# Hybrid two-layer block: buffer places on 512-byte lines, and the order of work in the four norm stretches

## The chip, the cores and the metric

One core of a Trainium2 chip runs the program. The metric is the device time of one execution in microseconds. Engines are named as in the profile: PE (TensorE matmuls), PEld (TensorE weight loads), DVE (VectorE), ACT (ScalarE), POOL (GpSimd), SP (SyncE, which issues the DMAs).

## The reference

Two transformer-like layers run one after the other on one sequence of 1024 tokens of width 1024, in float32. Each layer has this form, and each half of it ends in a norm stretch:

```
h   = rmsnorm(x, g_pre_mix);  proj = h @ w_in          # 53 (layer 1) or 54 (layer 2) column blocks of 128
y_* = mixers(proj)                                      # scan, short conv and attention; or band attention,
                                                        # gated recurrences and spatial gating
mix = (sum over branches of gate * (y @ w_branch)) @ w_out
x   = x + rmsnorm(mix, g_post_mix)                      # a norm stretch
h   = rmsnorm(x, g_pre_mlp)
x   = x + rmsnorm(mlp(h), g_post_mlp)                   # a norm stretch; hidden width 4096, or 2 x 2816 gated
```

`rmsnorm(x, g) = x * rsqrt(mean(x*x) + 1e-6) * g`, with the mean over the 1024 features of one token.

## The kernel before

**Layout.** Activations are transposed: features on the 128 partitions, tokens along the free dimension. A float32 activation block of 128 features is [128, 1024], 4096 bytes in each partition. The input of the large products is kept as a pair, `act_hi` (rounded) and `act_lo` (the rest), each [128, 8, 1024]. Other products stream `f1hh`/`f1hl` and `f2hh`/`f2hl` (the MLPs' hidden blocks), `m1h`/`m1l` and `m2h`/`m2l` (the merges of the mixers' outputs).

**Products.** A weight tile is split the same way into `w_hi` (ACT, L268) and `w_lo` (POOL, L272) from `w_raw`, which SP fetches in units of eight tiles. One tile of one output block is six matmuls on one PSUM pair: (w_hi, hi), (w_hi, lo), (w_lo, hi), each over two halves of 512 tokens. The weights stand still and the activations stream. `products` (L312) does this for whole stages. The class `TwoBlocks` (L431) does it for two output blocks by half, at chosen moments.

**How many.** Streams of 512 columns from `act_hi` and `act_lo`: layer 1's projection 53 blocks x 48 and layer 2's 54 x 48, together 5136; two output products `mix_out`, 384 each; the hidden products of the MLPs, 1536 and 2112. That makes 9552, of which 48 stand on L981. Streams from the other pairs: f1 1536, f2 1056, m1 576, m2 384, together 3552.

**Woven stages.** The projections are not stages of their own: `Woven` hands their tiles out one by one between the instructions of the mixers, by points counted in the code (`point(n)`) or by a time (`beside(us)`, with TILE_US = 1.42 for one tile). TensorE runs all of it in program order. From about 92 to 860 us the projection of layer 1 is woven with its mixers, from 1857 to 2620 us that of layer 2.

**Bridges.** Between two large products stands a norm stretch, `bridge`. It runs four times: after each `mix_out` (the first at about 1060 to 1124 us, the third at 2795 to 2857 us), after the first MLP (the second, 1802 to 1861 us), and after the second MLP (the last, which ends the program). It finishes the last two output blocks of the product before (`tail`), normalises by half of the tokens, and starts the first two blocks of the next product (`head`). For each half h and block k there is a `step(h, k)`: `add` on DVE (L519 and L520; on the last bridge L510 and L513 or L515), ACT's `act_hi` (L534), DVE's `act_lo` (L535), ACT's square (L539), then on PE the head's matmuls (L431) and the sum of the square over the features (L545). In the first half the head's second block follows two steps behind; in the second half it comes after the last step, eight tiles in a row.

The scale of a half needs the sum of the squares of all eight output blocks. ACT squares a block, POOL adds it to `squares` (L589), `half_sums` sums over the partitions on PE (L453, eight matmul records), `half_root` goes DVE (L467) and ACT (L468), and `half_spread` is DVE's reciprocal (L473) and PE's spread to all partitions (L475). For the second half these calls stand after step (0, 3), (0, 4) and (0, 6). On the last bridge they stand after (0, 2), (0, 4) and (0, 6), and there the last square is summed by PE itself, not through POOL.

The head's own scale comes the same way in L462 to L475. The evictions of its first half, `head.evicted(o, 0, ...)`, stand in DVE's and ACT's order after steps (1, 4) and (1, 5). What they do depends on the product: `relu2` (L1833, L1834, ACT L1829, L1830) on the first bridge, `first_rows` (L1926) on the second, `swiglu` (L1839, ACT L1841, L1843, L1830) on the third.

**Places.** Buffers in SBUF follow one another in the order in which they are allocated, each start rounded up to 32 bytes. The first one, `w_raw`, starts at byte 16512 of each partition. The start of a buffer modulo 512 bytes (slices of tiles and halves add multiples of 512 and change nothing):

| buffer | start | modulo 512 | modulo 256 |
|---|---|---|---|
| w_raw, w_hi, w_lo | 16512, 24704, 32896 | 128 | 128 |
| act_hi, act_lo | 43328, 76096 | 320 | 64 |
| m1h, m2h, f1hh, f2hh and their other halves | 121216 and on | 384 | 128 |
| foxks (streamed in the first attention) | 166272 | 384 | 128 |
| bandks (streamed in the band attention) | 158880 | 160 | 160 |

`sb` is the function that allocates.

Of the kernel before, what the change touches and what calls it, by code (L numbers as in the profile page):

```python
# [9 lines left out]
P = 128  # L10
# [41 lines left out]
for _name, _n in VEC_NAMES:  # L52
    VEC[_name] = sum(VEC[m][1] for m in VEC), _n
NVEC = sum(n for _, n in VEC_NAMES)


# [69 lines left out]
def _build(nc, ctx, t, out):  # L126
    def sb(at, name, shape, dt=F32):
        return at.enter_context(nc.sbuf_tensor(name, shape, dt))
# [93 lines left out]


    raw = sb(ctx, "w_raw", [P, 2, KT * P])
    whi = sb(ctx, "w_hi", [P, 2, KT * P], F32R)
    wlo = sb(ctx, "w_lo", [P, 2, KT * P], F32R)
    vec = sb(ctx, "vec", [P, NVEC])
    ident = sb(ctx, "ident", [P, P])
    causal = sb(ctx, "causal", [P, P])
    ones = sb(ctx, "ones", [P, P])  # L230
    pair = [ctx.enter_context(nc.psum_tensor(f"pair{i}", [P, L], F32)) for i in range(2)]
# [3 lines left out]
    act_lo = sb(ctx, "act_lo", [P, KT, L], F32R)  # L235
    tok = sb(ctx, "tok", [P, 2 * L // P])
    rs = sb(ctx, "rs", [P, L])
# [241 lines left out]
    def bridge(tail, tail_evict, y, squares, x, x_ready, sq, gain, out_dram, next_gain, head=None, head_evict=None,  # L479
# [26 lines left out]
        def add(h, k):  # L506

            yk, half = y[:, k, halves[h]], halves[h]
            if not next_gain:
                scaled = V.mark(V.after(y_scale[h], x_ready[k]).scalar_tensor_tensor(yk, yk, col(gain, k), bank[h][:],  # L510
                                                                                     ALU.mult, ALU.mult))
                if k in (1, 3, 5):
                    added[h, k] = G.mark(G.after(scaled, x_ready[k]).tensor_tensor(yk, yk, x(k)[:, half], ALU.add))  # L513
                else:
                    added[h, k] = V.mark(V.then().tensor_tensor(yk, yk, x(k)[:, half], ALU.add))  # L515
                SP.wait_ge(*added[h, k])
                stores[k % 2].mark(SP.dma_start(out_dram[k][:, half], yk))
                return
# [29 lines left out]
        for k in range(KT):  # L548
            step(0, k)
            if k == 0:  # L550
                tail.evicted(1, 1, tail_evict)
                summed = G.last()
            if k == 3 and next_gain:
                sums = half_sums(bank[1][:], squares[:, halves[1]], True, True, summed)
            if k == 2 and not next_gain:
                half_sums(bank[1][:], squares[:, halves[1]], True, False, summed)
                sums = half_sums(bank[1][:], last_square[0], False, True, last_square[1])
            if k == 4:
                root = half_root(1, bank[1][:], 1.0 / D, sums)
            if k == 6:  # L560
                y_scale[1] = half_spread(1, bank[1][:], root)
# [4 lines left out]
        for k in range(KT):  # L566
# [5 lines left out]
            if next_gain and k == 3:  # L572
                rs_ready = A.mark(A.after(spread).copy(rs[:, halves[0]], sides[0]))
            if next_gain and k in (4, 5):
                V.after(rs_ready)
                head.evicted(k - 4, 0, head_evict)
        if next_gain:
            root = half_root(3, sides[1], 1.0 / D, done[1][-1], rs[:, halves[1]])
            for k in range(KT - lag[1], KT):
                head.tile(1, 1, k)  # L580
            spread = half_spread(3, sides[1], root)
            V.after(A.mark(A.after(spread).copy(rs[:, halves[1]], sides[1])))
            for o in range(2):
                head.evicted(o, 1, head_evict)

    def square_sum(y, sq, squares, mark):
# [272 lines left out]
    def s5(first_two, first_evicts, w, stored):  # L859
# [3 lines left out]
        with ExitStack() as keep:  # L863
# [185 lines left out]
            for p0 in range(0, PAIRS, 8):  # L1049
# [3 lines left out]
                for _ in cmul(wp[:, RE, pr, :, :], wp[:, IM, pr, :, :], b_re, b_im, *a_pow, t0, t1):  # L1053
                    w.beside(1.7)
            wp_ready = V.last()
# [568 lines left out]
    def lru(at, ops, x, sp, freed):  # L1624

        r, ig, xc, la = (sb(at, "lr_" + n, [P, 2, L]) for n in ("r", "i", "xc", "la"))
        m, gate = x, la
# [171 lines left out]
    def mix_out(late, x_dram, gain, out_dram, next_gain, head_evict):  # L1799
# [16 lines left out]
        def tail_evict(o, half, psum, ready, read):  # L1816
            dst = y[:, 6 + o, half]
            square_sum(dst, sq[:, half], squares[:, half], read(A.after(ready).copy(dst, psum)))

        stage(3, 2, 2, KT, rhs, evict, per={A: 2, G: 2}, ahead=True)  # L1820
        bridge(TwoBlocks(KT, act_rhs, split=True), tail_evict, y, squares, lambda k: late.hl[:, k, :].bitcast(F32), x_ready,
               late.square_row, gain, out_dram, next_gain, TwoBlocks(KT, act_rhs), head_evict)

# [25 lines left out]
    def mlp(late, x_dram, gain, out_dram, next_gain, groups, gated, head_evict=None):  # L1849
# [25 lines left out]
        for n, tiles in enumerate(groups):  # L1875
# [22 lines left out]
            def tail_evict(o, half, psum, ready, read):  # L1898
                dst = acc[:, 6 + o, half]
                if not next_gain and o and half.start:  # L1900
                    a = read(V.after(ready).tensor_tensor(dst, dst, psum, ALU.add))
                    last_square.extend([sq[:, half], A.mark(A.after(a, G.last()).activation(sq[:, half], dst, ACT.Square))])
                    return
                square_sum(dst, sq[:, half], squares[:, half],
                           read(V.after(ready).tensor_tensor(dst, dst, psum, ALU.add)))

# [245 lines left out]
```

How the kernel before makes its waits and increments, by code:

```python
    def after(self, *marks):  # L71
        for m in marks:
            if m is not None:
                self.engine.wait_ge(m[0], m[1])
        return self.engine
# [136 lines left out]
    def barrier():  # L213
        marks = [x.last() for x in (V, A, G, PE, load, store, *loads, *stores)]
        if not background:
            marks += [x.last() for x in (*pair_read, *outs)] + [(s_mm, used["units"] + 2)]
        for e in (nc.vector, nc.scalar, nc.gpsimd, nc.sync):
            for s, n in marks:
                e.wait_ge(s, n)
# [43 lines left out]
    def split_unit(b, slot, fills, pieces=1):  # L265
        nc.scalar.wait_ge(s_raw[slot], 16 * fills)
        nc.scalar.wait_ge(s_mm, b + 1)
        nc.scalar.copy(whi[:, slot, :], raw[:, slot, :]).then_inc(s_whi, 1)
        nc.gpsimd.wait_ge(s_whi, b + 3)
        n = KT * P // pieces
        for at in range(0, KT * P, n):
            last = nc.gpsimd.tensor_tensor(wlo[:, slot, at:at + n], raw[:, slot, at:at + n],
                                           whi[:, slot, at:at + n].bitcast(F32), ALU.subtract)
        last.then_inc(s_split, 1)
# [1 line left out]
    def fetch_unit(b, slot):  # L276
        if not (isinstance(b, int) and b < 2):
            SP.wait_ge(s_split, b + 1)
        SP.dma_start(raw[:, slot, :], t["stream"][b]).then_inc(s_raw[slot], 16)
# [8 lines left out]
    def products(i, base, per_turn, n_out, tiles, rhs, evict, ahead=False):  # L288
# [16 lines left out]
                    nc.tensor.wait_ge(s_split, b + 3)  # L305
                if k == 0:
                    nc.tensor.wait_ge(reads.sem, reads.n)
                hi, lo = rhs(o, k)
```

## Time and profile before

| what | value |
|---|---|
| three runs, median (lowest to highest) | 3598.07 us (3594.38 to 3599.45) |
| the profiled execution, its own time | 3594.94 us |
| its span, first to last instruction | 3593.0 us |
| mean granted TensorE clock | 0.990 |
| PE busy | 3460.5 us, 16160 matmuls |
| DVE, ACT, POOL busy | 1423.0, 874.0, 906.7 us |

Busy time of PE is a union of overlapping matmuls: each record lasts longer than the distance to the next one, so the pace of a stream is read from the distance between starts in the timeline, and the busy share only tells whether PE stood still. The last column of a row names who ended an idle time before it.

### The profile page before, as it was taken

Reading aid. Unit: us, or ns where it says so; the run is one execution under the profiler, and the core shown is the slowest. Engines: PE = TensorE matmul, PEld = TensorE weight load, DVE = VectorE, ACT = ScalarE, POOL = GpSimd, SP = SyncE. Lnnn points to the kernel's source line nnn. Section 1 sums busy time; section 2 is a strip of 40 time slices with the busy share of each in tenths; the row PEclk is TensorE's granted clock in tenths of the full one; section 3 lists DMA queues with packets and bytes.
Section 4 is the critical chain, followed back from the end, with each engine's and each line's share of the span. In section 5 each row is a group of like instructions: output and inputs, shape, how many; then the busy total and the mean of one; then the engine's idle time right before and its main releaser. Section 6 shows DMA issues by size and latency. Waiting matters only on the chain.

```text
span 3593.0 us, 40675 instructions
## 1 busy us (share of the span) xinstructions
PE 3460.5 (96%) x16160; PEld 2794.4 (78%) x16160; DVE 1423.0 (40%) x1581; ACT 874.0 (24%) x1068; POOL 906.7 (25%) x455
## 2 busy tenths in 40 slices
PE   8999999999998999999989998999999899999997
PEld 6788877887876888888867886777777688888886
DVE  6733566555324121212153446564552521121123
ACT  3222223224322111111132222312342411111112
POOL 2211111112341222222322213331254222222224
PEclk9999999999999999999999999999999999999998
DMA  3535433315421111111224313213353111111113
GB/s 129 154 92 147 131 131 118 113 59 202 142 73 72 51 47 47 47 52 42 100 94 128 98 65 119 81 66 135 126 197 122 71 47 53 47 47 47 47 47 128
DMA packets 101600, 333.40 MB, mean 93 GB/s; under 512 B 11920, under 2 KB 21520, under 8 KB 101328
## 3 DMA queue, kind: packets, MB, share of 16 engines
q1 hardware_dynamic: 100896, 329.52, 27.7%
q8 instruction: 90, 1.47, 0.2%
q10 hardware_dynamic: 576, 2.10, 0.2%
q14 instruction: 38, 0.31, 0.0%
HBM read 249.06 MB, written 85.52 MB: 93 GB/s over the span
## 4 chain that ended last, share of the span: by engine, by line
PE 62%; DVE 4%; issue 1%; ACT 1%; DMA 0%; POOL 0%; SPq 0%; DVEq 0%; ACTq 0%; POOLq 0%
PE pair L312 55%; PE pair L431 3%; PE bank L751 1%; DVE hg_t L1417 1%; PE wide L545 1%; PE bank L626 0%; PE wide L788 0%; DVE act_lo L535 0%; PE bank L1427 0%; DVE bandr L762 0%; DVE f2y L510 0%; DVE hg_pt L1436 0%; PE wide L1427 0%; DVE p L1764 0%; DVE act_lo L1772 0%
## 5 line engine op out<-in xcount | busy, mean ns | idle before, releaser
L272 POOL TENSOR_TENSOR w_lo<-w_raw,w_hi 128x1024 fp32r<-128x1024 f32 (+1 forms) x304 | 690.6, 2276 | 2502.4 <-ACT w_hi L268 2502.1
L312 PE MATMUL pair<-act_hi,w_hi 128*128 128x512 f32 x2976 | 960.3, 404 | 11.8 <-DVE p L597 4.8
L312 PE MATMUL pair<-act_lo,w_hi 128*128 128x512 f32 x2976 | 937.8, 396 | 0.0
L312 PE MATMUL pair<-act_hi,w_lo 128*128 128x512 f32 x2976 | 937.2, 396 | 0.0
L312 PEld LDWEIGHTS pair<-act_lo,w_hi 128*128 128x128 f32 x2976 | 560.7, 188 | 136.9
L312 PEld LDWEIGHTS pair<-act_hi,w_lo 128*128 128x128 f32 x2976 | 560.0, 188 | 137.0
L312 PEld LDWEIGHTS pair<-act_hi,w_hi 128*128 128x128 f32 x2976 | 541.2, 189 | 132.5 <-issue 14.8
L268 ACT CAST w_hi<-w_raw 128x1024 fp32r<-128x1024 f32 x274 | 287.3, 1048 | 922.8 <-PE pair L312 871.3
L597 DVE TENSOR_TENSOR p<-pair,rs 128x1024 f32<-128x1024 f32 x100 | 122.2, 1223 | 370.1 <-PE pair L312 361.0
L1868 DVE TENSOR_TENSOR f2v<-pair,rs 128x1024 f32<-128x1024 f32 x42 | 51.4, 1225 | 346.5 <-PE pair L312 346.5
L312 PE MATMUL pair<-f1hh,w_hi 128*128 128x512 f32 x480 | 147.8, 389 | 0.0
L312 PE MATMUL pair<-f1hl,w_hi 128*128 128x512 f32 x480 | 147.8, 389 | 0.0
L312 PE MATMUL pair<-f1hh,w_lo 128*128 128x512 f32 x480 | 147.8, 389 | 0.0
L431 PE MATMUL pair<-act_hi,w_hi 128*128 128x512 f32 x192 | 88.3, 460 | 42.2 <-DVE act_lo L535 30.1
L1862 DVE TENSOR_TENSOR f1v<-pair,rs 128x1024 f32<-128x1024 f32 x30 | 36.8, 1225 | 195.8 <-PE pair L312 195.8
L1894 DVE TENSOR_TENSOR f1y<-f1y,pair 128x1024 f32 x22 | 26.9, 1221 | 201.4 <-PE pair L312 201.4
L312 PEld LDWEIGHTS pair<-f1hh,w_hi 128*128 128x128 f32 x480 | 90.1, 188 | 18.8
L312 PEld LDWEIGHTS pair<-f1hl,w_hi 128*128 128x128 f32 x480 | 90.1, 188 | 18.8
L312 PEld LDWEIGHTS pair<-f1hh,w_lo 128*128 128x128 f32 x480 | 90.1, 188 | 18.7
L312 PE MATMUL pair<-f2hh,w_hi 128*128 128x512 f32 x328 | 101.0, 389 | 0.0
L312 PE MATMUL pair<-f2hl,w_hi 128*128 128x512 f32 x328 | 101.0, 389 | 0.0
L1857 ACT CAST f1hh<-f1v 128x1024 f32 x30 | 31.5, 1049 | 285.7 <-DVE f1v L1863 285.7
(478 smaller groups left out, 4047.4 us busy)
## 6 DMA issues: line engine op xcount, KB each, us to landing
w_raw<-in_stream SPq DMA_DIRECT2D x275, 512.0 KB, 3.5
proj<-p SPq DMA_DIRECT2D x101, 512.0 KB, 2.6
m2g<-proj SPq DMA_DIRECT2D x32, 512.0 KB, 4.7
foxx<-proj SPq DMA_DIRECT2D x32, 256.0 KB, 5.2
m1g<-proj SPq DMA_DIRECT2D x16, 512.0 KB, 3.6
x<-f1y SPq DMA_DIRECT2D x16, 512.0 KB, 2.6
act_lo<-x SPq DMA_DIRECT2D x16, 512.0 KB, 7.2
fx_cb<-fox_cum SPq DMA_DIRECT2D x8, 512.0 KB, 6.7
```

What stands on the lines that cost most here:

```text
L268: nc.scalar.copy(whi[:, slot, :], raw[:, slot, :]).then_inc(s_whi, 1)
L272: last = nc.gpsimd.tensor_tensor(wlo[:, slot, at:at + n], raw[:, slot, at:at + n], whi[:, slot, at:at + n].bitcast(F32), ALU.subtract)
L312: last = nc.tensor.matmul(out_pair[:, h * HALF:(h + 1) * HALF], wt, a[:, h * HALF:(h + 1) * HALF], start=k == 0 and n_pass == 0, stop=k == ...
L431: last = nc.tensor.matmul(out, wt, a[:, half], start=k == 0 and n_pass == 0, stop=k == self.tiles - 1 and n_pass == 2)
L545: done[h].append(PE.mark(nc.tensor.matmul(sides[h], ones[:], sq(h, k % 2), start=k == 0, stop=k == KT - 1)))
L597: done = read(V.after(ready, stored).tensor_tensor(buf[:, slot, :], psum[:], rs[:], ALU.mult))
L751: last = nc.tensor.matmul(bank[1][:, n % 4 * P:(n % 4 + 1) * P], vt[:, h // 2 % 2, h % 2, k0 // P + j, :], pt[:, sl, j * P:(j + 1) * P], s ...
L1417: V.mark(nc.vector.tensor_tensor(t0[rows, sl, :, h, :].rearrange("p t (a w) -> p t a w", w=w), q4h, e4h, ALU.mult))
L1857: a = A.mark(A.after(mark).copy(hi, x[:, s, :]))
L1862: a = read(V.then(ready).tensor_tensor(x[:, s, :], psum[:], rs[:], ALU.mult))
L1868: v = read(V.then(ready).tensor_tensor(x[:, o, :], psum[:], rs[:], ALU.mult))
L1894: done = read(V.after(ready).tensor_tensor(dst, dst, psum[:], ALU.add))
```

## The change

1. `sb` first looks at where the next buffer would start. If the buffer has 512 bytes or more in each partition and the place is not a multiple of 512, it allocates a filler up to that multiple. `vec` (exempt) and `tok` (small) now come first, and `ident`, `causal` and `ones` before the weights. Four buffers of the gated recurrence keep the old rounding. With that, w_raw, w_hi, w_lo, act_hi, act_lo and all m1, m2, f1, f2 pairs start at a multiple of 512.
2. On all four bridges the square of the last output block's second half is summed on PE (`last_of`, a second `half_sums` call) and no longer added by POOL. The sums stand after step (0, 2), the root after (0, 3), the spread after (0, 5).
3. The head's first-half evictions stand behind the last step and behind the enqueuing of the eight last tiles: one before the last root, one between the root and the spread.
4. On the last bridge POOL does the residual addition for k = 0, 2, 4, 6 (before: 1, 3, 5), DVE the rest.
5. In the first mixer six calls of `beside` in each of two turns ask for 2 us in place of 1.7.

```diff
+LINE = 512
...
-    def sb(at, name, shape, dt=F32):
+    def sb(at, name, shape, dt=F32, line=LINE):
+        fill = -(-(-nc.sbuf_base // 32) * 32) % line // 4
+        if 4 * math.prod(shape[1:]) >= line and fill:
+            at.enter_context(nc.sbuf_tensor(name + "_fill", [P, fill], F32))
         return at.enter_context(nc.sbuf_tensor(name, shape, dt))
...
+    vec = sb(ctx, "vec", [P, NVEC], line=32)
+    tok = sb(ctx, "tok", [P, 2 * L // P])
+    ident = sb(ctx, "ident", [P, P])
+    causal = sb(ctx, "causal", [P, P])
+    ones = sb(ctx, "ones", [P, P])
     raw = sb(ctx, "w_raw", [P, 2, KT * P])
     whi = sb(ctx, "w_hi", [P, 2, KT * P], F32R)
     wlo = sb(ctx, "w_lo", [P, 2, KT * P], F32R)
-    vec = sb(ctx, "vec", [P, NVEC])
-    ident = sb(ctx, "ident", [P, P])
-    causal = sb(ctx, "causal", [P, P])
-    ones = sb(ctx, "ones", [P, P])
...
-                if k in (1, 3, 5):
+                if k in (0, 2, 4, 6):
                     added[h, k] = G.mark(G.after(scaled, x_ready[k]).tensor_tensor(yk, yk, x(k)[:, half], ALU.add))
...
-            if k == 3 and next_gain:
-                sums = half_sums(bank[1][:], squares[:, halves[1]], True, True, summed)
-            if k == 2 and not next_gain:
+            if k == 2:
                 half_sums(bank[1][:], squares[:, halves[1]], True, False, summed)
                 sums = half_sums(bank[1][:], last_square[0], False, True, last_square[1])
-            if k == 4:
+            if k == 3:
                 root = half_root(1, bank[1][:], 1.0 / D, sums)
-            if k == 6:
+            if k == 5:
                 y_scale[1] = half_spread(1, bank[1][:], root)
...
-            if next_gain and k in (4, 5):
-                V.after(rs_ready)
-                head.evicted(k - 4, 0, head_evict)
         if next_gain:
-            root = half_root(3, sides[1], 1.0 / D, done[1][-1], rs[:, halves[1]])
             for k in range(KT - lag[1], KT):
                 head.tile(1, 1, k)
+            V.after(rs_ready)
+            head.evicted(0, 0, head_evict)
+            root = half_root(3, sides[1], 1.0 / D, done[1][-1], rs[:, halves[1]])
+            head.evicted(1, 0, head_evict)
             spread = half_spread(3, sides[1], root)
...
+    def last_of(last, y, sq, mark):
+        last.extend([sq, A.mark(A.after(mark, G.last()).activation(sq, y, ACT.Square))])
...
-        r, ig, xc, la = (sb(at, "lr_" + n, [P, 2, L]) for n in ("r", "i", "xc", "la"))
+        r, ig, xc, la = (sb(at, "lr_" + n, [P, 2, L], line=32) for n in ("r", "i", "xc", "la"))
...
             dst = y[:, 6 + o, half]
-            square_sum(dst, sq[:, half], squares[:, half], read(A.after(ready).copy(dst, psum)))
+            a = read(A.after(ready).copy(dst, psum))
+            if o and half.start:
+                last_of(last_square, dst, sq[:, half], a)
+            else:
+                square_sum(dst, sq[:, half], squares[:, half], a)
...
-                    w.beside(1.7)
+                    w.beside(2)
```

## Rows read from the trace of the kernel before

**Rows 1.** The page: the span, TensorE's share of it.

```profile
span 3593.0 us, 40675 instructions
...
PE 3460.5 (96%) x16160; PEld 2794.4 (78%) x16160; DVE 1423.0 (40%) x1581; ACT 874.0 (24%) x1068; POOL 906.7 (25%) x455
```

**Rows 2.** The page, costliest groups: busy us, mean ns of one.

```profile
L312 PE MATMUL pair<-act_lo,w_hi 128*128 128x512 f32 x2976 | 937.8, 396 | 0.0
...
L312 PE MATMUL pair<-f1hh,w_hi 128*128 128x512 f32 x480 | 147.8, 389 | 0.0
```

**Rows 3.** Timeline, TensorE, streams of act_hi and act_lo: start us, us.

```profile
2899.23 0.63 PE L312 MATMUL pair<-act_hi,w_hi 128*128 128x512 f32 x2
...
2900.63 0.63 PE L312 MATMUL pair<-act_hi,w_hi 128*128 128x512 f32 x2
```

**Rows 4.** Timeline, TensorE, streams of f1hh and f1hl.

```profile
1399.76 0.62 PE L312 MATMUL pair<-f1hh,w_hi 128*128 128x512 f32 x2
...
1401.12 0.39 PE L312 MATMUL pair<-f1hh,w_hi 128*128 128x512 f32 x1
```

**Rows 5.** Timeline, TensorE: one stream each of foxks and bandks.

```profile
561.16 0.39 PE L788 MATMUL wide<-foxks,foxql 128*128 128x512 f32 x1
...
1942.21 0.39 PE L788 MATMUL wide<-bandks,bandql 128*128 128x512 f32 x1
```

**Rows 6.** Windows, TensorE: stretch, length, busy, (records), granted clock, DMA share, GB/s.

```profile
92.00:860.00 768.00, 741.12 (x3958) 0.99 0.40 125
...
1124.00:1787.00 663.00, 662.51 (x2880) 1.00 0.17 54
1857.00:2620.00 763.00, 733.00 (x3651) 0.99 0.30 103
2620.00:2704.00 84.00, 78.78 (x340) 1.00 0.62 219
2857.00:3550.00 693.00, 692.87 (x2997) 1.00 0.17 55
```

**Rows 7.** Chain of work that ended last, 1857 to 2620 us: shares by line.

```profile
by line: PE pair L312 64.9%; PE bank L751 3.1%; issue 2.8%; DVE hg_t L1417 2.4%; PE bank L626 2.2%; PE wide L788 2.0%; PE bank L1427 1.4%; DVE bandr L762 1.3%; DVE hg_pt L1436 1.2%; PE wide L1427 1.2%; DMA hg_g<-proj 1.0%; DVE hg_t L1419 0.
```

**Rows 8.** Timeline, TensorE, the merge of the second block.

```profile
2632.50 0.73 PE L312 MATMUL pair<-m2h,w_hi 128*128 128x512 f32 x2 [0.79 <-DVE p L1757]
```

**Rows 9.** Timeline, VectorE, the first bridge, second half begins.

```profile
1087.81 0.69 DVE L519 TENSOR_TENSOR f1y<-f1y,bank 128x512 f32<-128x512 f32 x1 [2.83 <-PE bank L475]
...
1091.25 0.68 DVE L462 TENSOR_TENSOR rs<-wide,ident 128x512 f32<-128x512 f32 x1
```

**Rows 10.** Timeline, TensorE, the same bridge: the sums over squares, the last step.

```profile
1078.86 0.95 PE L453 MATMUL bank<-ones,f1ss 128*128 128x1 f32 x8
...
1089.02 1.02 PE L545 MATMUL wide<-f1v,ones 128*128 128x512 f32 x2
```

**Rows 11.** Timeline, VectorE, first bridge, steps with the first evictions.

```profile
1100.99 0.75 DVE L535 SCALAR_TENSOR_TENSOR act_lo<-f1y,vec,act_hi 128x512 fp32r<-128x512 f32 x1 [0.55 <-ACT act_hi L534]
...
1105.93 0.75 DVE L535 SCALAR_TENSOR_TENSOR act_lo<-f1y,vec,act_hi 128x512 fp32r<-128x512 f32 x1
...
1110.86 0.75 DVE L535 SCALAR_TENSOR_TENSOR act_lo<-f1y,vec,act_hi 128x512 fp32r<-128x512 f32 x1
```

**Rows 12.** Timeline, TensorE, the same steps.

```profile
1111.66 0.80 PE L431 MATMUL pair<-act_hi,w_hi 128*128 128x512 f32 x1 [2.83 <-DVE act_lo L535]
1112.25 0.63 PE L431 MATMUL pair<-act_lo,w_hi 128*128 128x512 f32 x1
```

**Rows 13.** Timeline, VectorE, the third bridge, the same steps.

```profile
2835.40 0.75 DVE L535 SCALAR_TENSOR_TENSOR act_lo<-f2y,vec,act_hi 128x512 fp32r<-128x512 f32 x1 [0.55 <-ACT act_hi L534]
...
2843.42 0.75 DVE L535 SCALAR_TENSOR_TENSOR act_lo<-f2y,vec,act_hi 128x512 fp32r<-128x512 f32 x1
```

**Rows 14.** Timeline, VectorE, the second bridge, the same steps.

```profile
1845.51 0.68 DVE L1926 TENSOR_TENSOR f1v<-pair,rs 128x512 f32<-128x512 f32 x1
```

**Rows 15.** Timeline, VectorE, the last bridge.

```profile
3579.94 0.75 DVE L510 SCALAR_TENSOR_TENSOR f2y<-f2y,vec,bank 128x512 f32<-128x512 f32 x1 [2.17 <-PE bank L475]
```

More of the change, by code:

```diff
@@ L235, in _build @@
     act_lo = sb(ctx, "act_lo", [P, KT, L], F32R)
-    tok = sb(ctx, "tok", [P, 2 * L // P])
     rs = sb(ctx, "rs", [P, L])
@@ L1817, in tail_evict @@
             dst = y[:, 6 + o, half]
-            square_sum(dst, sq[:, half], squares[:, half], read(A.after(ready).copy(dst, psum)))
+            a = read(A.after(ready).copy(dst, psum))
[3 more added lines that the diff above has]
+                square_sum(dst, sq[:, half], squares[:, half], a)
         stage(3, 2, 2, KT, rhs, evict, per={A: 2, G: 2}, ahead=True)
+        last_square = []
         bridge(TwoBlocks(KT, act_rhs, split=True), tail_evict, y, squares, lambda k: late.hl[:, k, :].bitcast(F32), x_ready,
-               late.square_row, gain, out_dram, next_gain, TwoBlocks(KT, act_rhs), head_evict)
+               late.square_row, gain, out_dram, next_gain, TwoBlocks(KT, act_rhs), head_evict, last_square)
     def first_hidden(late, gated):
@@ L1899, in tail_evict @@
                 dst = acc[:, 6 + o, half]
[L1900 to L1905, printed above, removed]
+                v = read(V.after(ready).tensor_tensor(dst, dst, psum, ALU.add))
+                if o and half.start:
+                    last_of(last_square, dst, sq[:, half], v)
+                else:
+                    square_sum(dst, sq[:, half], squares[:, half], v)
             def hidden_rhs(o, k, last=hidden_last, tiles=tiles):
```

## The prediction

> **What bounds the kernel now.** The page comes first: TensorE is busy for 3460.5 of 3593.0 us [rows 1], and no other engine for half of that. So only two things can shorten the program: less standing still (132 us in all), or a faster pace while TensorE runs. A busy share can't show pace, because the records overlap. The timeline can. In the middle of a hidden product, starts of `act_hi` and `act_lo` streams stand at 2899.23 and 2900.63 us with six streams between them: 1.40 / 6 = 233.3 ns for one [rows 3]. Streams of `f1hh` and `f1hl` stand at 1399.76 and 1401.12: 1.36 / 6 = 226.7 ns [rows 4]. The page's means of one record differ by the same 7 ns (396 and 389) [rows 2]. Both stretches run at the full granted clock, 1.00 [rows 6], both stream 512 columns, with the same weight buffers and outputs. At 2.4 GHz these are 560 and 544 cycles, 48 and 32 more than the 512 columns.
>
> The windows then tell where pace counts in full: 662.5 of 663 us busy in the first MLP, 692.9 of 693 in the second, but 741 of 768 and 733 of 763 in the two woven stretches [rows 6]. The chain of waits through the second woven stretch has the product line with 64.9% [rows 7], 495 us. Its 2496 projection streams take 582 us at 233.3 ns, so about 0.85 of them are on the chain. Last, the timelines of the bridges show TensorE waiting for VectorE's `act_lo`.
>
> **The places.** What differs between the two streams is where they start. A row of [128, 512] from `act_hi` starts 64 bytes past a multiple of 256; one from `f1hh` 128 bytes past. To the next multiple of 256 that leaves 192 and 128 bytes, which are 48 and 32 float32 columns: exactly the two surpluses. With a start on a multiple of 512 this reading leaves none, 512 cycles or 213.3 ns. Two points do not make a rule. Another reading is that a start off a multiple of 128 costs 6.7 ns and that the other 13.3 ns belong to this kind of stream; then 226.7 ns is the end. A third pair of rows weighs a little: `bandks` starts 160 bytes past (24 columns), off every multiple of 64, and its record of 0.39 us is no longer than that of `foxks`, which starts where `f1hh` does [rows 5]. Under "off 128 costs more" it should be longer. I take 215 ns, between 213.3 and 226.7 and near the end that the exact match points at, with 1.7 ns left for what does not overlap.
>
> Per stream that saves 18.3 ns on `act_*` and 11.7 ns on the other pairs.
>
> - `act_*` outside the woven stretches: 9552 - 5136 = 4416 streams. 288 are heads on the three bridges, where VectorE sets the step; half of their saving is counted. 4128 x 18.3 = 75.5 us, 144 x 18.3 = 2.6.
> - f1, f2 and m1: 3168 x 11.7 = 37.1 us. The 384 of m2 give nothing: TensorE waits for VectorE's evictions there [rows 8] and stands still for 5 of 84 us [rows 6].
> - Woven: 5136 x 18.3 = 94.0 us. The filler between the mixers' steps gets shorter, and where a mixer's chain is on the path, it only waits longer. At most 0.85 is kept [rows 7]; as TILE_US and the points are laid for tiles of 1.4 us, further waits will open, so I keep 0.6, 56 us, with 0.35 as the low bound.
>
> Together 171 us. For other engines no row shows a price of places, and it is taken as nothing.
>
> The Trainium skill (TensorE: Matmul & The Clock Gate, "Wait — 56ns, not 53.3ns?") gives back-to-back matmuls of N columns a start distance of N / 2.4 GHz plus about 2.5 ns, 215.7 ns at 512. Neither stream here reaches it (226.7 and 233.3). By it the sum of the three items would be an estimated 164 us, and nothing in it says that a place is what is missing.
>
> **The bridges.** *First-half evictions.* On the first bridge two `act_lo` with a `relu2` eviction before each stand 1110.86 - 1100.99 = 9.87 us apart [rows 11]; two plain steps, each three VectorE instructions of 0.7, take 4.2. Taking the evictions out gives 5.7 us. On the third it is 8.02 - 4.2 = 3.8 [rows 13]; on the second two instructions of 0.68, 1.3 [rows 14]. They now run behind the last step, beside eight tiles of TensorE (24 streams, 5.2 us, and 2 us of the step's own matmuls before them). There VectorE and ScalarE need 2.8 for an eviction, 1.6 for the root, 2.8 for the next and 0.2 for the reciprocal: 7.4 against 7.2 of cover. ScalarE's split of the next weights stands in front of the first eviction's copy. I charge 0.5 us each on the first and third; without cover it would be up to 5.6 each, and the step would be a wash. The long waits also let the clock fall: after standing still for 2.83 us a stream's record lasts 0.63 us, not 0.40 [rows 12]. That goes with the wait, 2 us for all bridges.
>
> *Last square on TensorE, earlier root and spread.* One more `half_sums` is eight records, 0.95 us [rows 10], on each of three bridges. It goes on TensorE in the half where TensorE and VectorE are nearly even, so I count it in full. VectorE's idle time of 2.83 us before the second half [rows 9] goes, but its root at 1091.25 [rows 9] needs the last sum of the first half, which ends at 1089.02 + 1.02 = 1090.04 [rows 10]. So the lead is 1.2 us, and 0.3 net; for three bridges 1. Nothing queues behind GpSimd's missing addition.
>
> *Last bridge.* VectorE waits 2.17 us for the spread [rows 15]; one `add` (1.4 us) now stands between reciprocal and wait. Per half one residual addition of 0.7 moves to GpSimd. Together 2.8 us, right ahead of the end.
>
> Sum: 5.7 + 3.8 + 1.3 - 1.0 + 2 + 1 + 2.8 = 16 us, bounds 8 and 22. `beside(2)` brings 12 x 0.3 / 1.42 = 2.5 tiles forward; the tiles are the same, so nothing.
>
> **Sum.** 171 + 16 = 187 us off the profiled execution's 3594.9 us gives 3408. The runs' median lies 3 us higher, so **3410 us**.
>
> **Rivals.**
>
> *A step at 128 only* (pace ends at 226.7): 4128 x 6.67 + 144 x 6.67 = 28.5, woven 34 x 0.7 = 24, bridges 16: 68 us, 3530 us. For it: the two-point fit could be chance. Against: rows 5.
>
> *Places do nothing*: the two paces come from something else that goes with these buffers. Only the bridges stay: 3582 us. The Trainium skill (SBUF — State Buffer, Specifications) speaks of lines of 16 bytes; all starts here are multiples of 32 already, and by that the change of place would give nothing. Rows 3 and 4 leave that page without a reason for their 7 ns.
>
> *Slower: the common line hurts.* Before, weights (128 past a multiple of 512), `act_*` (320) and `f1hh` (384) start at different places in a 512-byte line; after, all at 0. If a weight load and the stream beside it, or a stream and another engine's write, then meet in the same part of the memory, the pace rises. Priced by the only step that the rows show, 6.7 ns more for every stream: (4272 + 3168) x 6.67 = 50, woven 34 x 0.85 = 29, less 16: 63 us slower, 3661 us. It decides from about 1.3 ns a stream, where it has eaten the 16 us. Against it: the weights and `f1hh` are only 256 apart already, and rows 4 are the faster ones.
>
> **Chances.** 215 ns or near 0.62; step at 128 0.18; nothing 0.11; slower 0.05; the pace is gained but most woven saving is lost and a bridge breaks even (3455 to 3480 us) 0.04. In the likeliest case the pace may be 213.3 with 0.85 kept and 22 us on the bridges (85 + 42 + 87 + 22 = 236 us, 3362) or 216.5 with 0.35 and 8 (69 + 32 + 30 + 8 = 139, 3459); that is its own range. The whole range takes in the step at 128: 3360 to 3535. A measurement of this kernel tells 0.2%, 7 us, from no change. Faster 0.91, same 0.03, slower 0.06: "nothing" is still 16 us faster unless its bridges fail.
>
> **What would show it.** Starts of `act_hi` streams 215 ns apart and equal to those of `f1hh` (record means near 377 in both groups): the place is the cause. 389 in both: the step at 128. 396 and 389 as now: nothing. Longer: the slower rival. In the woven stretches more and longer waits of TensorE for VectorE and ScalarE, its busy share falling to about 93%. On the bridges no `act_lo` pair 4.9 us apart, and the first matmul of the next stage about 10 us after the last `act_lo`. Wrong would make it above all a pace between 217 and 226, which no row excludes, and mixers whose chains were hardly hidden.

## The result, and the profile after

The changed kernel takes 3534.73 us (median of 4 runs, 3532.25 to 3539.94) against 3597.09 (median of 4, 3594.38 to 3599.45): a ratio of 0.9829, 95% interval 0.9812 to 0.9846. That is 62 us, where 187 were forecast, and it lies 5 us from the rival "a step at 128 only" (3530). The experiments show that this rival came near the right time for a wrong reason.

The page, costliest groups, answers [rows 1, 2]:

```profile
span 3532.2 us, 40721 instructions
...
PE 3412.5 (97%) x16184; PEld 2799.5 (79%) x16184; DVE 1425.0 (40%) x1579; ACT 873.6 (25%) x1068; POOL 913.2 (26%) x454
...
L318 PE MATMUL pair<-act_lo,w_hi 128*128 128x512 f32 x2976 | 924.0, 392 | 0.0
...
L318 PE MATMUL pair<-f1hh,w_hi 128*128 128x512 f32 x480 | 147.8, 389 | 0.0
```

The `f1` record has not moved at all; the `act` record fell from 396 to 392, and no further than 389 where it runs undisturbed. The timeline of TensorE in the second MLP has the same six streams as [rows 3]:

```profile
2899.23 0.61 PE L318 MATMUL pair<-act_hi,w_hi 128*128 128x512 f32 x2
...
2900.59 0.61 PE L318 MATMUL pair<-act_hi,w_hi 128*128 128x512 f32 x2
```

1.36 / 6 = 226.7 ns, the pace that `f1` had before [rows 4] and still has. Windows of TensorE by stage (columns as in [rows 6]): first MLP, second woven stretch, second MLP.

```profile
1102.91:1757.40 654.49, 654.49 (x2880) 1.00 0.17 55
1829.96:2578.40 748.44, 718.31 (x3608) 0.98 0.30 104
...
2812.06:3492.00 679.94, 679.94 (x3000) 1.00 0.17 56
```

Cut at the first stream of each stage, the two timelines give the table below. Its two last columns are the differences to the kernel before of the experiments `places_only` and `bridges_only`, from their own profiles.

| stage | before | after | after - before | places alone | bridges alone |
|---|---|---|---|---|---|
| start and first head | 52.4 | 51.4 | -1.0 | -1.0 | -0.5 |
| woven 1, to its last stream | 785.5 | 773.4 | -12.0 | -5.9 | -2.6 |
| to the first mix_out | 137.6 | 138.7 | +1.1 | +0.9 | +0.4 |
| mix_out, both | 134.4 | 130.6 | -3.8 | -3.8 | 0.0 |
| bridge 1 | 81.8 | 74.0 | -7.8 | -2.3 | -6.2 |
| MLP 1 | 662.6 | 654.5 | -8.1 | -9.7 | 0.0 |
| bridge 2 | 75.2 | 72.5 | -2.7 | -0.2 | -2.5 |
| woven 2, to its last stream | 752.6 | 748.4 | -4.2 | -6.0 | +2.0 |
| to the second mix_out | 95.0 | 94.9 | 0.0 | 0.0 | +0.2 |
| bridge 3 | 80.1 | 73.5 | -6.6 | +1.0 | -6.1 |
| MLP 2 | 693.6 | 680.1 | -13.5 | -13.5 | 0.0 |
| last bridge | 42.3 | 40.0 | -2.2 | 0.0 | -2.2 |
| span | 3593.0 | 3532.2 | -60.8 | -40.6 | -17.4 |

These are single executions. The two woven stretches together vary most from one to the next: in the profiles of the eight kernels at distance 0 (explained below) with the old `TILE_US`, they are 11 to 20 us shorter than before, 16 in the changed kernel's own.

The bridges in VectorE's timeline, first bridge. The first row answers [rows 9], the last two [rows 11]:

```profile
1071.19 0.69 DVE L525 TENSOR_TENSOR f1y<-f1y,bank 128x512 f32<-128x512 f32 x1 [0.68 <-PE bank L481]
...
1075.70 0.69 DVE L468 TENSOR_TENSOR rs<-wide,ident 128x512 f32<-128x512 f32 x1 [0.99 <-PE wide L551]
...
1087.49 0.74 DVE L541 SCALAR_TENSOR_TENSOR act_lo<-f1y,vec,act_hi 128x512 fp32r<-128x512 f32 x1
...
1089.54 1.62 DVE L541 SCALAR_TENSOR_TENSOR act_lo<-f1y,vec,act_hi 128x512 fp32r<-128x512 f32 x2
```

The wait of 2.83 us ahead of the second half is now 0.68 us, with 0.99 us for the last sum of the first half behind it; from 1078.61 us on the steps' `act_lo` follow one another every 2.05 to 2.67 us, and no pair is 4.9 us apart. The end of the same bridge on TensorE:

```profile
1100.35 1.16 PE L481 MATMUL wide<-ident,tok 128*128 128x128 f32 x8 [1.17 <-DVE tok L479]
1102.91 1.15 PE L318 MATMUL pair<-act_hi,w_hi 128*128 128x512 f32 x2 [1.40 <-DVE f1v L1846]
...
1106.41 0.65 PE L318 MATMUL pair<-act_lo,w_hi 128*128 128x512 f32 x2
```

TensorE stands still for 1.17 us, because the reciprocal (1100.13) queues behind the second eviction on VectorE (ScalarE's root was done at 1097.62), and for 1.40 us as before. In this execution the granted clock is 0.5 for 3.4 us after that: two streams' record lasts 1.15 us there and 0.65 at 1106.41, and this is the 1.6 us by which MLP 1 gained less than with the places alone.

### The profile page after: what moved, and what is told of

Read it like the earlier page. It is cut to its first block and busy times, and to the rows that moved or that the text cites. A ratio compares the mean times of both kernels' runs of the same rounds, so it can differ in the third digit from the quotient of the medians.

```text
span 3532.2 us, 40721 instructions
## 1 busy us (share of the span) xinstructions
PE 3412.5 (97%) x16184; PEld 2799.5 (79%) x16184; DVE 1425.0 (40%) x1579; ACT 873.6 (25%) x1068; POOL 913.2 (26%) x454
## 5 line engine op out<-in xcount | busy, mean ns | idle before, releaser
L278 POOL TENSOR_TENSOR w_lo<-w_raw,w_hi 128x1024 fp32r<-128x1024 f32 (+1 forms) x304 | 698.6, 2302 | 2441.4 <-ACT w_hi L274 2441.1
L318 PE MATMUL pair<-act_hi,w_hi 128*128 128x512 f32 x2976 | 946.2, 399 | 11.2 <-DVE p L605 4.8
L318 PE MATMUL pair<-act_lo,w_hi 128*128 128x512 f32 x2976 | 924.0, 392 | 0.0
L318 PE MATMUL pair<-act_hi,w_lo 128*128 128x512 f32 x2976 | 921.6, 391 | 0.0
L1881 DVE TENSOR_TENSOR f2v<-pair,rs 128x1024 f32<-128x1024 f32 x42 | 51.4, 1224 | 332.8 <-PE pair L318 332.8
L437 PE MATMUL pair<-act_hi,w_hi 128*128 128x512 f32 x192 | 85.8, 447 | 26.4 <-DVE act_lo L541 14.0
L1907 DVE TENSOR_TENSOR f1y<-f1y,pair 128x1024 f32 x22 | 26.9, 1221 | 201.3 <-PE pair L318 201.3
L318 PE MATMUL pair<-f2hh,w_lo 128*128 128x512 f32 x328 | 101.0, 389 | 0.0
```

The costliest lines, as they stand in the source:

```text
L278: last = nc.gpsimd.tensor_tensor(wlo[:, slot, at:at + n], raw[:, slot, at:at + n], whi[:, slot, at:at + n].bitcast(F32), ALU.subtract)
L318: last = nc.tensor.matmul(out_pair[:, h * HALF:(h + 1) * HALF], wt, a[:, h * HALF:(h + 1) * HALF], start=k == 0 and n_pass == 0, stop=k == ...
L437: last = nc.tensor.matmul(out, wt, a[:, half], start=k == 0 and n_pass == 0, stop=k == self.tiles - 1 and n_pass == 2)
L1881: v = read(V.then(ready).tensor_tensor(x[:, o, :], psum[:], rs[:], ALU.mult))
L1907: done = read(V.after(ready).tensor_tensor(dst, dst, psum[:], ALU.add))
```

## The experiments

**First call: the two halves of the change, and the rule of the places.**

`places_only` is the kernel before with part 1 of the diff and nothing else. `bridges_only` is the changed kernel with `sb` and the order of allocation of before.

> The kernel before with the changed places alone (part 1 of the change), bridges and the six calls of beside as before. Theory A, the places give the act streams 6.7 ns each outside the woven stretches (4128 of them, 27 us) and less inside: the time falls by 40 us, to about 3557, with steady starts of act streams 226.7 ns apart, and with the woven stretches 12 and 4 us shorter as in the changed kernel. Rival B, the woven stretches owe their gain to the six calls of beside or to the bridges: then only the 27 us remain here, about 3570.

> Parts 2 to 5 of the change on the places of before. Theory A, the bridges are worth about what the prediction gave them, 16 us: about 3581, with act streams still 233.3 ns apart and bridges about 7, 2, 6 and 2 us shorter. Rival B, the shorter bridges of the changed kernel owe half of their gain to the faster streams on them: about 3589.

`places_only`: 3551.91 us, ratio 0.9868 (0.9853 to 0.9883). `bridges_only`: 3576.45 us, ratio 0.9934 (0.9921 to 0.9948). In both the stages go as theory A had them: with the places alone the products outside the woven stretches gain 27.0 us (9.7 + 13.5 + 3.8), which is what the whole change gives them but for the 1.6 us at half clock in MLP 1; with the bridges alone `act` streams keep their record of 396 ns and the four bridges give 6.2 + 2.5 + 6.1 + 2.2 = 17.0 us. Of the first woven stretch's 12 us the places alone gave 5.9, less than A said: the stretch takes 779.6 us there, 771.6 to 776.7 in the seven like kernels with the shorter bridges. The difference was not explained (`beside_17` below rules out part 5). As medians the parts are 47 and 22 us and add up to 69, against 62 together; each interval is about 5 us to either side, and the profiles' spans add up to 58.0 of 60.8, so nothing shows that the parts help or harm each other.

```diff
 # line128
-LINE = 512
+LINE = 128
 # act_at_64, on top of line128 (PLACE is 0 for every other buffer)
+PLACE = {"act_hi": 64, "act_lo": 64}
-        fill = -(-(-nc.sbuf_base // 32) * 32) % line // 4
+        fill = (PLACE.get(name, 0) + -(-(-nc.sbuf_base // 32) * 32)) % line // 4
```

> The changed kernel with fillers up to a multiple of 128 bytes in place of 512: act_hi and act_lo then start 384 past a multiple of 512, the weights 256 past. Theory A, only the place modulo 128 counts: streams at 226.7 ns everywhere, the same time as the changed kernel, 3535. Rival B, a place modulo 256 or 512 counts as well: act streams between 226.7 and 233.3 ns apart, up to 3575.

> The kernel with fillers up to 128 bytes, but act_hi and act_lo 64 bytes further, 64 past a multiple of 128 as before; all else stays at multiples of 128. Theory A, the place of the streamed operand alone sets its pace: act streams 233.3 ns apart again, f1 and f2 streams 226.7, 40 us over the changed kernel, about 3575. Rival B, the weights or the places of other buffers had set the pace: act streams stay at 226.7 ns, about 3535.

`line128`: 3535.65 us, 0.9823 (0.9808 to 0.9838), 226.7 ns everywhere, as A had it. `act_at_64`: 3567.08 us, 0.9913 (0.9898 to 0.9928), and with its rows both theories fall. TensorE's timeline, `act` streams in the second MLP and `f1` streams in the first:

```profile
2899.65 0.62 PE L319 MATMUL pair<-act_hi,w_hi 128*128 128x512 f32 x2
...
2901.02 0.62 PE L319 MATMUL pair<-act_hi,w_hi 128*128 128x512 f32 x2
```

```profile
1200.48 0.64 PE L319 MATMUL pair<-f1hh,w_hi 128*128 128x512 f32 x2
...
1201.88 0.63 PE L319 MATMUL pair<-f1hh,w_hi 128*128 128x512 f32 x2
```

The `act` streams, moved back to 64 past a multiple of 128, are not at 233.3 ns but at 1.37 / 6 = 228.9 (mean over MLP 2; the rows are rounded to 10 ns), and the `f1` streams, which lie at a multiple of 512 as in the changed kernel, are slow: 232.4 ns (1.40 / 6 here). So the place of the streamed buffer is not what counts. What had changed for `f1` is where its weights lie: 384 past a multiple of 512, no longer 0. Written as the distance from weights to stream, all runs so far fall in line:

| kernel | w_hi, w_lo (mod 512) | act | distance, pace | f1, f2, m1 | distance, pace |
|---|---|---|---|---|---|
| before | 128 | 320 | 192, 233.3 ns | 384 | 256, 226.7 ns |
| changed | 0 | 0 | 0, 226.7 | 0 | 0, 226.7 |
| line128 | 384 | 384 | 0, 226.7 | 384 | 0, 226.7 |
| act_at_64 | 384 | 448 | 64, 228.9 | 0 | 128, 232.4 |

(The expectation of `line128` has the weights at 256; with `vec`, `tok` and the three small buffers ahead of them they lie at 384.)

**Second call: the distance by itself, and the parts of the bridges.** `weights_at_64` has `PLACE = {"w_hi": 64, "w_lo": 64}`. `pace_probe` adds this behind the last store:

```python
for start, cols, w_start in PROBES:
    for n in range(48):
        tile, step, h = n // 6 % 6, n // 2 % 3, n % 2
        w0, a0 = tile * P + w_start, tile * L + h * HALF + start
        nc.tensor.matmul(wide[:, h * HALF:h * HALF + cols], w_flat[step // 2][:, w0:w0 + P],
                         flat_act[:, a0:a0 + cols], start=True, stop=True)
    nc.tensor.matmul(wide[:, 0:64], w_flat[0][:, 0:P], flat_act[:, 0:64], start=True, stop=True)
```

> Fillers up to 128 bytes, but w_hi and w_lo 64 further: they start 448 past a multiple of 512, act_hi, act_lo, f1, f2 and m1 pairs 0 past one. So every streamed buffer lies 64 bytes past its weights modulo 256. Theory R (new, after act_at_64): the distance between stream and weights modulo 256 sets the pace, 0: 226.7, 64: 228.9, 128: 232.4, 192: 233.3 ns; then all streams here stand 228.9 ns apart. Theory A (the place of the streamed operand alone): 226.7 ns for all. Rival W (the place of the weights alone, off a multiple of 128): one other pace for all, 232 or more.

> The changed kernel, and behind its last store 24 groups of 48 streams with the product's pattern of weights, read from act_hi and w_hi or w_lo, each group with its own shift in bytes of the stream and of the weights. Nothing is left out of the computation; the end is some 270 us later. Theory R, only the distance modulo 256 counts: stream shifts of 0, 64, 128, 192, 256, 512 bytes give 226.7, 228.9, 232.4, 233.3, 226.7, 226.7 ns; weights shifted by 64 with the stream at 0 give 233.3 (distance 192), by 192 give 228.9, by 256 give 226.7; both shifted by 64 or both by 128 give 226.7. Rival H, the reading of the prediction (columns up to the next multiple of 256 are paid extra, weights don't matter): stream shifts alone set the pace, shifts of the weights change nothing. With 256 columns at distance 0 the start distance is 106.7 ns plus the same 13.3 if the surplus is per stream, or 113.3 if it grows with the columns.

`weights_at_64` (one execution, 3550.07 us): `f1` streams that lie where they lay in the changed kernel are slower, by the shift of the weights alone, 1.37 / 6, mean 228.9 ns, as are the `act` streams. Theory R had that, A and W had not.

```profile
1199.79 0.62 PE L319 MATMUL pair<-f1hh,w_hi 128*128 128x512 f32 x2
...
1201.16 0.62 PE L319 MATMUL pair<-f1hh,w_hi 128*128 128x512 f32 x2
```

`pace_probe`: each row is the 64-column marker at the end of a group, so the time between two rows is one group of 48 streams. Between the first and the last marker shown, 14 groups in order: the stream shifted by 64, 96, 128, 160, 192, 224, 256, 384 and 512 bytes, the weights by 64, 128, 192 and 256, and both by 64.

```profile
3573.28 0.19 PE L2072 MATMUL wide<-act_hi,w_hi 128*128 128x64 f32 x1
...
3584.38 0.19 PE L2072 MATMUL wide<-act_hi,w_hi 128*128 128x64 f32 x1
...
3595.70 0.19 PE L2072 MATMUL wide<-act_hi,w_hi 128*128 128x64 f32 x1
...
3606.95 0.20 PE L2072 MATMUL wide<-act_hi,w_hi 128*128 128x64 f32 x1
...
3618.30 0.19 PE L2072 MATMUL wide<-act_hi,w_hi 128*128 128x64 f32 x1
...
3629.62 0.19 PE L2072 MATMUL wide<-act_hi,w_hi 128*128 128x64 f32 x1
...
3640.92 0.19 PE L2072 MATMUL wide<-act_hi,w_hi 128*128 128x64 f32 x1
...
3651.93 0.19 PE L2072 MATMUL wide<-act_hi,w_hi 128*128 128x64 f32 x1
...
3663.22 0.19 PE L2072 MATMUL wide<-act_hi,w_hi 128*128 128x64 f32 x1
...
3674.23 0.19 PE L2072 MATMUL wide<-act_hi,w_hi 128*128 128x64 f32 x1
...
3685.54 0.19 PE L2072 MATMUL wide<-act_hi,w_hi 128*128 128x64 f32 x1
...
3696.85 0.19 PE L2072 MATMUL wide<-act_hi,w_hi 128*128 128x64 f32 x1
...
3707.97 0.19 PE L2072 MATMUL wide<-act_hi,w_hi 128*128 128x64 f32 x1
...
3718.99 0.19 PE L2072 MATMUL wide<-act_hi,w_hi 128*128 128x64 f32 x1
...
3730.03 0.19 PE L2072 MATMUL wide<-act_hi,w_hi 128*128 128x64 f32 x1
```

A group takes 11.01 to 11.04 us at distances 0, 256 and 512 however they are made, weights shifted (3718.99 - 3707.97) or both (3730.03 - 3718.99) included, and 11.10 to 11.35 at all others. The mean of its last 29 start distances, once the stream has settled:

| distance, bytes | 0 | 16 | 32 | 48 | 64 | 96 | 128 | 160 | 192 | 224 | 256 | 320 | 384 | 448 |
|---|---|---|---|---|---|---|---|---|---|---|---|---|---|---|
| ns, stream shifted | 226.7 | 231.8 | 233.3 | 230.0 | 228.9 | 233.2 | 232.3 | 234.4 | 233.3 | 233.3 | 226.7 | | 233.5 | |
| ns, weights shifted | | | | | | | | | | | 226.7 | 229.0 | 233.5 | 233.2 |

Both shifted by 64 or by 128: 226.7; stream by 192 and weights by 64 (distance 128): 232.7. Weights shifted by 64 change the pace and equal shifts of both do not, which settles R against H. Whether the pattern repeats every 256 or every 512 bytes stays open: distances 256 apart agree within 0.2 ns except 128 and 384 (232.3 and 233.5), and 384 itself gave 232.4 in another group of the last probe. No distance gives less than 226.7. With 384 and 496 columns at distance 0 it is 173.3 and 223.3 ns, 13.3 and 16.7 over the columns at 2.4 GHz, so the surplus goes with the stream and hardly with its columns.

For the bridges, `evictions_back` puts the first-half evictions back after steps (1, 4) and (1, 5) and the root ahead of the last tiles; `last_square_back` puts the last square back on POOL and sums, root and spread one step later:

```diff
 # evictions_back
+            if next_gain and k in (4, 5):
+                V.after(rs_ready)
+                head.evicted(k - 4, 0, head_evict)
 # last_square_back
-            if k == 2:
+            if k == 3 and next_gain:
+                sums = half_sums(bank[1][:], squares[:, halves[1]], True, True, summed)
+            if k == 2 and not next_gain:
```

> The changed kernel with the first-half evictions back after steps (1, 4) and (1, 5) (part 3 undone). By the prediction part 3 gave 5.7 - 0.5 us on the first bridge, 3.8 - 0.5 on the third, 1.3 on the second, and about 2 of clock: the bridges get 5, 3.5 and 1.5 us longer, some 10 in all, 3545. Rival: the evictions only moved their cost to behind the last step, where TensorE stands still for 2.6 us before the next product: less than 3 us in all, 3537.

> The changed kernel with the last square on POOL and the sums, root and spread one step later, on the three inner bridges (part 2 undone there; the last bridge keeps it). By the prediction part 2 gave 0.3 us net on each: 3536. Rival: the earlier scale takes away VectorE's 2.8 us of waiting before the second half, and what was called a wait that TensorE covers was on the path: 2 us a bridge, 3541.

`evictions_back`: 3541.44 us, 0.9850 (0.9833 to 0.9866). By the stages of its profile the three bridges are 4.3, 1.2 and 3.0 us longer, 8.5 in all, near the 9.8 of the prediction without the clock and clear of the rival's 3. VectorE's steps with an eviction between them are 4.93 us apart again:

```profile
1092.13 0.75 DVE L541 SCALAR_TENSOR_TENSOR act_lo<-f1y,vec,act_hi 128x512 fp32r<-128x512 f32 x1
...
1097.06 1.63 DVE L541 SCALAR_TENSOR_TENSOR act_lo<-f1y,vec,act_hi 128x512 fp32r<-128x512 f32 x2
```

`last_square_back`: 3535.98 us, 0.9832 (0.9816 to 0.9849); the median can't tell it from the changed kernel, the stages can: 1.7, 1.3 and 1.3 us longer on the inner bridges, nearer to the rival's 2 than to the prediction's 0.3. The 1.7 is of a bridge with 3.4 us at the half granted clock (from 1057.4), the two 1.3 are not. VectorE's wait is back:

```profile
1073.86 0.69 DVE L525 TENSOR_TENSOR f1y<-f1y,bank 128x512 f32<-128x512 f32 x1 [2.82 <-PE bank L481]
```

On the last bridge it keeps the square on TensorE but has root and spread one step later, and that alone costs 2.0 of the 2.2 us gained there.

**Third call: the rule used, and the woven stretches.**

```diff
 # tok_line_moved, on the kernel before: one line, 64 bytes in each partition
+    tok = sb(ctx, "tok", [P, 2 * L // P])
     act_hi = sb(ctx, "act_hi", [P, KT, L], F32R)
     act_lo = sb(ctx, "act_lo", [P, KT, L], F32R)
-    tok = sb(ctx, "tok", [P, 2 * L // P])
 # tile_us_136, on the changed kernel
-TILE_US = 1.42
+TILE_US = 1.36
 # beside_17, on the changed kernel
-                    w.beside(2)
+                    w.beside(1.7)
```

> The kernel before with one line moved: tok, 64 bytes long, is allocated ahead of act_hi and not behind act_lo. act_hi and act_lo then start 64 bytes further, 384 past a multiple of 512 in place of 320, and nothing else moves; the weights stay at 128. Theory R: the distance of the act streams to their weights goes from 192 to 256 modulo 512, and all streams run at 226.7 ns, with no buffer of the products at a multiple of 512: the same gain as all the places of the change, 47 us, 3552. Rival L (a multiple of 512 is needed, or the other buffers' new places give part of the 47 us): less, between 3560 and 3598.

> The changed kernel with TILE_US = 1.36 (six streams of 226.7 ns) in place of 1.42: the calls of beside hand out 4% more tiles. The prediction said that the woven stretches keep only part of the saving because tiles are laid for 1.4 us. If so, the first woven stretch, which goes by beside, gets 3 to 8 us shorter, 3530. Rival: the kept part is set by the mixers' own chain and by the slower first streams after each interruption, and nothing changes, 3535.

> The changed kernel with 1.7 us again in the six calls of beside (part 5 undone). The prediction counted part 5 as nothing: 3535. Rival: in the changed kernel the first woven stretch was 6 us shorter than with the places alone, and this is part 5's: 3541.

`tok_line_moved`: 3553.41 us, 0.9879 (0.9862 to 0.9895), the same as all the places together (0.9868, 0.9853 to 0.9883). MLP 1 and 2 and both `mix_out` are as long as in `places_only` to 0.01 us. Its `act` streams:

```profile
2899.00 0.62 PE L312 MATMUL pair<-act_hi,w_lo 128*128 128x512 f32 x2
...
2900.36 0.62 PE L312 MATMUL pair<-act_hi,w_lo 128*128 128x512 f32 x2
```

`tile_us_136`: 3543.50 us, 0.9856 (0.9840 to 0.9873), no gain. In its profile, the fastest of the four executions (3535.25), the first woven stretch is 12.3 us longer and the second 8.5 us shorter than in the changed kernel. Both theories missed that; where the 12 us come from was not followed. `beside_17`: 3534.84 us, 0.9833 (0.9817 to 0.9850), the first woven stretch 2.1 us longer, which is within its spread, the time the same: part 5 can't be measured, as predicted.

**Last call: other widths.** `width_probe` is the first probe with other groups; where it says one weight tile, all 48 streams load the same tile.

> The changed kernel, and behind its last store 24 more groups of 48 streams, made as in the first probe. Nothing is left out of the computation; the end is some 200 us later. In order: 128 columns with the stream shifted by 0, 64, 128, 192, 256, 320, 384, 448 bytes; 256 columns with the same eight; 512 columns with 0, 192, 320, 448; 512 columns with one and the same weight tile all along with 0, 192, 384; 256 columns with one weight tile and 0. Theory R as the first probe left it (distance modulo 512, 0 and 256 are best for 512 columns): 512 columns give 226.7, 233.3, 229.0, 233.2 ns; the first probe's 256 columns at 192 were 2.2 ns faster than at 0, so for narrow streams the order of the distances may turn; at 128 columns the load of the weights, 64 columns' time or more, may hide all differences. If the surplus of 13.3 ns belongs to reading other weights while a stream runs, the groups with one weight tile are nearer to 213.3 ns; if it belongs to every load of weights, the same 226.7.

The first eight groups, 128 columns, ran at half the granted clock and show 213.3 ns at every distance. The windows row, and the markers around the groups of 256 columns at 64, 128 and 192:

```profile
3538.00:3608.00 70.00, 70.00 (x330) 0.50 0.00 1
```

```profile
3618.33 0.19 PE L2073 MATMUL wide<-act_hi,w_hi 128*128 128x64 f32 x1
...
3624.09 0.19 PE L2073 MATMUL wide<-act_hi,w_hi 128*128 128x64 f32 x1
...
3629.96 0.20 PE L2073 MATMUL wide<-act_hi,w_hi 128*128 128x64 f32 x1
...
3635.54 0.19 PE L2073 MATMUL wide<-act_hi,w_hi 128*128 128x64 f32 x1
```

For 256 columns the order turns: 120.1 ns at 0 (its group began at the half clock), 117.8 at 64, 120.0 at 128, 113.3 at 192, and the same four again at 256 to 448. The rows show it: 5.58 us for the group at 192 (3629.96 to 3635.54), 5.76 at 64, 5.87 at 128. But the first probe had a group of 256 columns at 192 as well, from the same buffers, and it held 117.8 ns to its end, 5.77 us in all:

```profile
3758.20 0.20 PE L2072 MATMUL wide<-act_hi,w_hi 128*128 128x64 f32 x1
...
3763.97 0.19 PE L2072 MATMUL wide<-act_hi,w_hi 128*128 128x64 f32 x1
```

So the distance alone does not fix the pace of 256 columns; what else does was not found. For 512 columns all four distances come out as in the first probe to 0.3 ns (226.7, 233.5, 229.0, 233.5), and with one weight tile all along 0, 192 and 384 give 226.7, 233.4 and 232.4: the surplus does not need a change of weights. Each of these streams still loads its tile; streams without a load between them were not run, so it isn't shown that the 13.3 ns at the best distance come from the load.

## Why the prediction was wrong, point by point

- **What bounds the kernel**: right. TensorE's pace and its waits are all that moved.
- **The places, the rule**: this is the step that failed. It read the two paces of before as "columns up to the next multiple of 256" of the streamed buffer, from two rows that fitted exactly, and took 215 ns. What counts is the distance between the weights' place and the stream's, and before the change it was 256 for `f1`, `f2` and `m1`, already the best there is, and 192 for `act` (shown by `act_at_64`, `weights_at_64`, the probe and `tok_line_moved`). The exact match was chance. The text had the relation of weights and stream in its hands, but only as a rival in which a common line hurts.
- **The sizes from it**: f1, f2 and m1 gave 0 in place of 37.1 us; `act` outside the woven stretches 27.0 in place of 75.5 (4032 streams by 6.67 ns are 26.9; the rest stand on the bridges).
- **The rival "step at 128"**: its pace was right (226.7), its rule was not: `act_at_64` has buffers at multiples of 128 that stream at 232.4 ns. The row of `bandks` [rows 5], which spoke against it, is one isolated record and told nothing of pace. The Trainium skill (TensorE: Matmul & The Clock Gate, "Wait — 56ns, not 53.3ns?") gives 215.7 ns for 512 columns; no distance, width or reuse of weights tried here comes to it with these float32 operands, the lowest being 226.7.
- **The woven stretches**: 56 us predicted, 15 measured (12.0 - 1.1 + 4.2 + 0.0); at 6.67 ns a stream the step would have given 34 x 0.6 = 20, so the failed rule is most of it. Two things can have taken the rest, which is no larger than the spread of these stretches. First, after each interruption by other matmuls the streams start at a slower pace, and settle after some: in the first woven stretch of the changed kernel six streams take 1.39 us here (648.25 to 649.64) and 1.36 there (652.58 to 653.94).

```profile
648.25 0.63 PE L318 MATMUL pair<-act_lo,w_hi 128*128 128x512 f32 x2
...
649.64 0.62 PE L318 MATMUL pair<-act_lo,w_hi 128*128 128x512 f32 x2
...
652.58 0.62 PE L318 MATMUL pair<-act_lo,w_hi 128*128 128x512 f32 x2
...
653.94 0.62 PE L318 MATMUL pair<-act_lo,w_hi 128*128 128x512 f32 x2
```

  The mean distance of neighbouring `act` streams went from 233.3 to 228.5 ns in the first stretch and to 227.8 in the second. Over 5136 streams that is some 26 us less of TensorE, of which 15 arrived: the kept share of 0.6 (16 us of 26) was about right. TensorE is busy for 96.0% of the second woven stretch and was for 96.2% before; 93% was the sign for the larger saving. Second, the clock: summed over the stretches with a granted clock of 0.5, TensorE spent 17.1 us of the second woven stretch there before, 30.7 after. The probe kernel, which is the changed one up to its end, had 23.9 us and took 745.2 us for the stretch instead of 748.4. Nine profiles of kernels with distance 0 or 256 lie between 20.5 and 34.1 us, the four with other distances between 13.7 and 20.5; `tile_us_136` has 10.2 us and the shortest stretch, 740.0; `tok_line_moved`, with the 34.1, has 750.0. That shorter streams leave longer pauses, which pull the clock down, would explain it, but is only argued.
- **The bridges**: right in sum, 16 us predicted, 17.0 with the bridges alone. Within it the evictions were worth 8.5, not 9.8, and their price behind the last step was 1.17 and 0.60 us of standing still on bridges 1 and 3, not 0.5 each. On bridge 1 it is 8.9 us from the first eviction (1091.26) to the reciprocal, where 2.8 + 1.6 + 2.8 = 7.2 were counted: the first eviction alone took 4.0, because VectorE waited 1.88 us for ScalarE's copy, which stood behind the split of the next weights. The prediction named that order and gave it no time. The earlier scale was worth 1.3 us a bridge, not 0.3: the wait of 2.83 us [rows 9] became 0.68 + 0.99, which is the lead of 1.2 us that the prediction had. So the 0.95 us that it charged for the eight extra records did not show; that VectorE and not TensorE sets the step there would explain it. The last bridge gave 2.2 of 2.8: VectorE still waits 0.36 us for the spread ([rows 15]: 2.17).

```profile
3519.29 1.41 DVE L516 SCALAR_TENSOR_TENSOR f2y<-f2y,vec,bank 128x512 f32<-128x512 f32 x2 [0.36 <-PE bank L481]
```

- **The clock on the bridges**: 2 us were counted, and no run settles them. The profile before has 6.8 and 3.4 us at half clock on bridges 1 and 3, the one after none, but 3.4 us right behind bridge 1 that cost 1.6; the probe kernel, the same up to its end, has none there. `beside_17`, which changes nothing on the bridges, has 3.4 us on each of the two and takes 1.2 and 1.1 us longer on them. In the row that the prediction read [rows 12] the clock had fallen at 1108.1 us, ahead of the wait of 2.83 us that it names; the standing still before the fall is the one of 3.11 us up to 1106.73.
- **A count**: of the 288 heads, 96 (the second bridge's) belong to the 5136 woven streams, not to the 4416. It is worth under 1 us. The sum of the low bound (69) leaves out the 2.4 us of the heads.
- **What would show it**: the sign named for the step at 128 (389 ns in both records) came, for `act` where nothing interrupts it. No pair of `act_lo` is 4.9 us apart, as forecast. The first product of the MLP starts 11.8 us after the last `act_lo`, not 10.
- **The bounds**: the low end of the places, 226.7 ns, was in the rows, and the time would have followed from it; 0.18 was too little for it against a fit of two points.

## What to carry to other kernels

Where one engine reads two operands at once, look at their places as a pair: a table of start modulo 512 for weights and streams, and their difference, costs nothing, and here one line (64 bytes of `tok` moved) was worth as much as realigning every buffer. For 512 float32 columns take a distance of 0 or 256 bytes; for 256 columns measure in the kernel itself, since 0 and 256 were never the best there and one distance showed two paces. And before a rule is built on two paces, test it on a kernel that moves the one operand and then the other.

## What was not expected of the hardware

- The start distance of TensorE's float32 streams depends on the distance in bytes between weights and stream, with a period of 512 or perhaps 256: 226.7 to 234.4 ns for 512 columns. For 256 columns it is 113.3 to 120.1 ns, and the distance alone does not fix it (117.8 and 113.3 both at 192). The Trainium skill (SBUF — State Buffer, "A bandwidth-pool intuition that's wrong (but worth ruling out)") names a second, independent read port for loads of weights; the probe's 226.7 against 233.2 ns, with only the weights moved, shows that the streams' pace still depends on where the weights lie. Whether the two reads meet in the memory was not measured.
- In the eight groups at the half granted clock (1.2 GHz) no distance made a difference, and 128 columns took 213.3 ns; the first streams of 256 columns behind them, still at that clock, stand 213 to 214 ns apart as well.
- After an interruption the streams keep a slower pace for up to some ten streams even at the best distance, so short bursts gain less than a long product.
